# Turning attention probabilities in 32x32 squares on VectorE and through DRAM, and multiplying them with v two subtiles at a time

## What is computed

```python
h = rms_norm(x, ln_g); proj = h @ w_in
# 8 query heads of 64, 2 key/value heads, blocks of 128 tokens, window of 128 keys
scores = einsum('bnqkgd,bnskd->bnkgqs', q * 64**-0.5, keys_of_this_and_previous_block)
scores = where(valid, scores - slope_h * distance, -1e30)
p = softmax(concat([scores, sink_h]))[..., :-1]          # each row sees exactly 128 keys
y_attn = einsum('bnkgqs,bnskd->bnqkgd', p, v) * silu(g_attn)
x = x + concat([y_pool, y_conv, y_attn]) @ w_out
out = rms_norm(x, final_g)
```

## Time and profile before

| | before |
|---|---|
| runs, us | 1399.31, 1399.58, 1400.87 |
| median | 1399.58 |
| the profiled execution's span | 1398.6 (the page gives no other time for it; 1.0 below the median) |
| busy: PE, DVE, ACT, POOL | 1376.3, 1189.1, 553.6, 389.1 us |
| attention stage | 0 to 617 us, eight blocks; blocks 1 to 5 take 73.3 us each |
| memory traffic | 114.27 MB read, 81.79 MB written |

### The profile page before, as it was taken

How to read it: one execution, slowest core, us unless ns; L and a number is a source line. 1 busy time by engine, 2 the same in 40 slices (tenths; PEclk the granted TensorE clock), 3 DMA queues, 4 the chain that set the end, 5 groups by cost and what they waited for, 6 DMA issues and landing times.

```text
span 1398.6 us, 21036 instructions
## 1 busy us (share of the span) xinstructions
PE 1376.3 (98%) x7326; PEld 1131.5 (81%) x7326; DVE 1189.1 (85%) x2480; ACT 553.6 (40%) x1435; POOL 389.1 (28%) x592
## 2 busy tenths in 40 slices
PE   6999999999999999999999999999999999999997
PEld 4888888888888888878888888888888888888886
DVE  5887878796978786769899998988999998898886
ACT  5756565655565654512212122111231333333332
POOL 5133324233242423120101101010010455445551
PEclk9999999999999999999999999999999999999999
DMA  9716070616252426363303213032326484555431
GB/s 216 206 45 257 19 273 19 235 75 207 95 199 103 151 106 210 123 118 153 136 16 136 101 66 135 15 135 101 125 113 260 201 264 161 177 180 171 159 108 74
DMA packets 89385, 197.23 MB, mean 141 GB/s; under 512 B 13904, under 2 KB 55248, under 8 KB 81616
## 3 DMA queue, kind: packets, MB, share of 16 engines
q1 hardware_dynamic: 65152, 172.28, 34.9%
q10 hardware_dynamic: 24144, 23.80, 6.5%
HBM read 114.27 MB, written 81.79 MB: 140 GB/s over the span
## 4 chain that ended last, share of the span: by engine, by line
PE 90%; DVE 7%; DMA 1%; ACT 1%; issue 1%; POOL 0%; SPq 0%; POOLq 0%; DVEq 0%; ACTq 0%
PE wide L346 13%; PE wide L347 13%; PE wide L348 13%; PE pair L1186 6%; PE pair L1187 6%; PE pair L1192 6%; PE wide L1186 4%; PE wide L1187 4%; PE wide L1192 4%; DVE m_tail L1967 3%; PE wide L1224 2%; PE pair L1157 2%; PE turn L1144 2%; PE turn L346 2%; PE pair L346 2%; PE pair L348 2%
## 5 line engine op out<-in xcount | busy, mean ns | idle before, releaser
L1967 DVE SCALAR_TENSOR_TENSOR m_tail<-m_tail,m_taps 128x512 f32<-128x512 f32 x480 | 338.4, 750 | 4.6
L108 POOL TENSOR_TENSOR pool_carrier<-pool_carrier 128x1 f32<-128x1 f32 x77 | 29.5, 383 | 692.0 <-DVE m_meanvar L1976 398.4
L1186 PE MATMUL pair<-xT,w_hi 128*128 128x512 f32 x384 | 154.0, 401 | 4.8 <-DVE w_lo L410 4.6
L1187 PE MATMUL pair<-xT,w_lo 128*128 128x512 f32 x384 | 150.6, 392 | 0.0
L1710 POOL TENSOR_TENSOR operand_sums<-m_y 128x512 f32<-128x512 f32 x75 | 102.0, 1360 | 167.8 <-PE wide L348 116.7
L1192 PE MATMUL pair<-xT,w_hi 128*128 128x512 f32 x384 | 147.1, 392 | 0.0
L787 POOL TENSOR_SCALAR a_rows<-a_rows,a_inv 128x128 f32<-128x128 f32 x256 | 111.4, 453 | 75.3 <-DVE a_inv L993 75.3
L346 PE MATMUL wide<-x_first,w_hi 128*128 128x512 f32 x320 | 125.5, 392 | 0.0
L346 PE MATMUL wide<-xT,w_hi 128*128 128x512 f32 x320 | 125.2, 391 | 0.0
L348 PE MATMUL wide<-x_first,w_hi 128*128 128x512 f32 x320 | 124.6, 389 | 0.0
L347 PE MATMUL wide<-x_first,w_lo 128*128 128x512 f32 x320 | 124.6, 389 | 0.0
(11 more groups left out here) (264 smaller groups left out, 3220.0 us busy)
## 6 DMA issues: line engine op xcount, KB each, us to landing
xT_scratch<-xT SPq DMA_DIRECT2D x16, 2048.0 KB, 8.2
x_first<-xT_scratch SPq DMA_DIRECT2D x16, 1024.0 KB, 7.6
xT<-xT_scratch SPq DMA_DIRECT2D x16, 1024.0 KB, 9.0
combo_scratch<-stage SPq DMA_DIRECT2D x28, 512.0 KB, 4.4
m_y<-y_scratch ACTq DMA_DIRECT2D x14, 1024.0 KB, 6.7
xs<-in_x_dram SPq DMA_DIRECT2D x20, 512.0 KB, 8.1
y_scratch<-y_out SPq DMA_DIRECT2D x8, 1024.0 KB, 4.2
y_scratch<-y_out SPq DMA_DIRECT2D x16, 512.0 KB, 2.9
```

The lines of the kernel that those rows point to most:

```text
L1186: nc.tensor.matmul(out, w.hi(c)[:, kk, cols], st.hi[:, kk, :], start=(kk == 0), stop=False)
L1187: nc.tensor.matmul(out, w.lo(c)[:, kk, cols], st.hi[:, kk, :], start=False, stop=False)
L1967: nc.vector.scalar_tensor_tensor(out=conv[:, i, :], in0=h[:, i, j:j + TB], scalar=taps[:, i, j:j + 1], in1=conv[:, i, :], op0=ALU.mult, op ...
```

## The change

The probabilities of a subtile are no longer turned on PE. Their tile is laid out as four runs of 32 keys, each with all heads. DVE transposes it in place in 32x32 squares (one instruction over 128x1024); SP stores the tile in DRAM (512 KB) and loads it back in four pieces of 32 partitions (128 KB each, runs of 1 KB), which puts the squares in their places. Where a key's row and a query lie in different halves of 64, the row belongs to one of the two key tiles alone and needs no mask. Where they lie in the same half, two instructions a subtile on POOL (rows 0 to 63, `mask_early`) and two on DVE (rows 64 to 127, `mask_late`) multiply with masks, over 512 elements a row each. `attend` takes two subtiles at once (32 matmuls) and writes the two banks `turn`; the products of a block's subtiles 0 and 1 come behind the next block's q0, those of 2 and 3 behind its v. `output` multiplies with the gate while copying, so `gate_output` on POOL and an ACT copy go. The slots o0 to o3 of the pair banks go. v is turned in the scores of subtile 1 instead of 0. SP's queue gets the stores and loads, and two of its other stores swap places. POOL's loop over the blocks is written out. In the last block the products of subtiles 0 and 1 come behind g3, and those of 2 and 3 behind ca0; DVE begins the mixer stage with their output.

```diff
@@ -576,7 +576,7 @@
     rows = sb("rows", [P, 4, D])
     k_hi = sb("k_hi", [P, KV, P + TB], F32R)
     k_lo = sb("k_lo", [P, KV, P + TB], F32R)
-    pT = sb("pT", [P, 2, KV, GROUP * P])
+    pT = sb("pT", [P, 2 * D])
     v = sb("v", [P, 1 + SUB, P])
     q_at = region.at
     q = sb("q", [P, HEADS, TB], F32R)
...
-           tanh.rearrange("p a b -> p (a b)"), pT[:, 0].rearrange("p b c -> p (b c)"), ident, ident_ready, first_rows)
...
+           tanh.rearrange("p a b -> p (a b)"), pT[:, D + D // 2:], ident, ident_ready, first_rows)
+    SQ = 32
+    RUNS = P // SQ
+    probs = [rows[:, b].rearrange("p (s h c) -> p h s c", s=RUNS, h=HEADS) for b in range(2)]
...
+    upper = rows[:, 2:4].rearrange("p a b -> p (a b)")
+    whole = [pT[:, 0:D], upper[:, 0:D]]
+    rest = [pT[:, D:D + D // 2], upper[:, D:D + D // 2]]
+    masks = upper[:, D + D // 2:]
+    earlier_tile, absent = masks[:, 0:P], masks[:, P:2 * P]
+    rest_mask, whole_mask = masks[:, 2 * P:2 * P + HD], masks[:, 2 * P + HD:3 * P]
...
-        use = PAIRED.index(p)
-        return len(PAIRED) // 2 * n + use // 2 - use % 2
+        return len(PAIRED) // 2 * n + PAIRED.index(p) // 2
+    def batches_before(n, batch):
+        return 2 * n + batch
...
+    def store_probs(sp, n, j):
+        m, b = SUB * n + j, j % 2
+        sp.wait_ge(squares_turned, m + 1)
+        need(sp, p_loaded[b], 16 * RUNS * (m // 2))
+        sp.dma_start(p_scratch[b], rows[:, b]).then_inc(p_stored[b], 16)
+    def load_probs(sp, n, j):
+        m, b = SUB * n + j, j % 2
+        sp.wait_ge(p_stored[b], 16 * (m // 2) + 16)
+        need(sp, pv_full, batches_before(n, j // 2))
+        squares = p_scratch[b].rearrange("(a r) (s e) -> s r a e", r=SQ, s=RUNS)
+        for s in range(RUNS):
+            sp.dma_start(whole[b][s * SQ:(s + 1) * SQ].rearrange("r (a e) -> r a e", a=RUNS), squares[s]
+                         ).then_inc(p_loaded[b], 16)
...
+                store_probs(sp, n - 1, 3)
                 st.load(sp, n + 1, (0, 1))
+                for j in (2, 3):
+                    load_probs(sp, n - 1, j)
             st.wait_loaded(sp, n + 1)
             if n == 0:
                 combos.load_raw(sp, 0, [(0, 1), (1, 1), (0, 0), (1, 0)])
             store_xT(n, 0)
             for s in combos.of_block(n, (0, 1)):
                 combos.store(sp, s)
+            store_xT(n, 1)
+            for s in combos.of_block(n, (2, 3, 4)):
+                combos.store(sp, s)
             if n > 0:
                 store(n - 1)
-            for s in combos.of_block(n, (2, 3, 4)):
-                combos.store(sp, s)
-            store_xT(n, 1)
+            for j in (0, 1):
+                store_probs(sp, n, j)
+                load_probs(sp, n, j)
+            store_probs(sp, n, 2)
...
+        for j in (2, 3):
+            load_probs(sp, NB - 2, j)
...
-            m, b = 4 * n + j, j % 2
+            m, b = SUB * n + j, j % 2
             for kv in range(KV):
-                carrier.pool_wait(pool, den_step, 4 * m + 2 * kv + 2)
+                pool.wait_ge(den_step, 4 * m + 2 * kv + 2)
                 for t in range(GROUP):
                     h = kv * GROUP + t
-                    last = nc.gpsimd.tensor_scalar(probs[:, b, h, :], probs[:, b, h, :], inv[:, b, h:h + 1], 0.5,
+                    last = nc.gpsimd.tensor_scalar(probs[b][:, h], probs[b][:, h], inv[:, b, h:h + 1], 0.5,
                                                    ALU.mult, ALU.mult)
                 last.then_inc(probs_ready, 1)
-        def gate_output(n, at):
-            pool.wait_ge(free(at[1]), earlier(*at) + 1)
-            pool.wait_ge(free(slot("o2")), earlier(n, slot("o2")) + 1)
-            for t in range(GROUP):
-                last = nc.gpsimd.tensor_tensor(y[:, t, :], y[:, t, :], gate[:, t, :], ALU.mult)
-            last.then_inc(gated, 1)
+        def mask_early(n, j):
+            m, b = SUB * n + j, j % 2
+            pool.wait_ge(p_loaded[b], 16 * RUNS * (m // 2 + 1))
+            part = runs(whole[b][:, 0:D // 2], halves[0])
+            nc.gpsimd.tensor_tensor(runs(rest[b], halves[0]), part, over_heads(rest_mask, halves[0]), ALU.mult)
+            nc.gpsimd.tensor_tensor(part, part, over_heads(whole_mask, halves[0]), ALU.mult).then_inc(masked, 1)
         def body(n):
-            if isinstance(n, int) and n == 0:
+            if n == 0:
                 make_seen()
-            if not isinstance(n, int) or n < NB - 1:
+            else:
+                mask_early(n - 1, 1)
+            if n < NB - 1:
                 st.root(pool, n + 1, carrier)
-            if not isinstance(n, int) or n > 0:
-                gate_output(n - 1, (n, slot("o3")))
+            if n > 0:
+                for j in (2, 3):
+                    mask_early(n - 1, j)
             for j in range(SUB):
                 normalise(n, j)
-        body(0)
-        with pool.Fori(1, NB - 1) as n:
+                if j == 2:
+                    mask_early(n, 0)
+                    if n == NB - 1:
+                        mask_early(n, 1)
+        for n in range(NB):
             body(n)
-        body(NB - 1)
+        for j in (2, 3):
+            mask_early(NB - 1, j)
...
-        def pT_copy(m, kv):
-            dve.wait_ge(p_turned, 2 * m + kv + 1)
-            if isinstance(m, int) and m == 0:
-                dve.wait_ge(seen_ready, 3)
-            for tile in range(2):
-                last = nc.vector.tensor_tensor(pT[:, tile, kv, :], turn[kv][:], seen[:, tile], ALU.mult)
-            last.then_inc(pT_done, 1)
+        def turn_squares_of_probs(m):
+            dve.wait_ge(probs_ready, 2 * m + 2)
+            nc.vector.transpose(rows[:, m % 2], rows[:, m % 2]).then_inc(squares_turned, 1)
...
-                pT_copy(4 * n - 1, 0)
-                pT_copy(4 * n - 1, 1)
+                turn_squares_of_probs(SUB * n - 1)
+                mask_late(dve, n - 1, 1)
...
+                output(dve, n - 1, 0)
...
                 make_combos(n, (t,) if t < 3 else (3, 4))
+                if t > 1 and not first:
+                    mask_late(dve, n - 1, t)
...
+            if not first:
+                output(dve, n - 1, 1)
             for j in range(SUB):
-                for kv in range(KV):
-                    take_scores(n, j, kv)
-                    if kv == 0 and j:
-                        pT_copy(4 * n + j - 1, 0)
-                        pT_copy(4 * n + j - 1, 1)
+                take_scores(n, j, 0)
+                if j in (1, 2):
+                    turn_squares_of_probs(SUB * n + j - 1)
+                elif j == 3:
+                    mask_late(dve, n, 0)
+                    if final:
+                        mask_late(dve, n, 1)
+                take_scores(n, j, 1)
                 invert(4 * n + j, j % 2, 0)
+                if j == 3:
+                    turn_squares_of_probs(SUB * n + 2)
...
+        turn_squares_of_probs(SUB * NB - 1)
+        output(dve, NB - 1, 0)
+        for j in (2, 3):
+            mask_late(dve, NB - 1, j)
+    def mask_late(dve, n, j):
+        m, b = SUB * n + j, j % 2
+        dve.wait_ge(p_loaded[b], 16 * RUNS * (m // 2 + 1))
+        part = runs(whole[b][:, D // 2:], halves[1])
+        nc.vector.tensor_tensor(runs(rest[b], halves[1]), part, over_heads(rest_mask, halves[1]), ALU.mult)
+        nc.vector.tensor_tensor(part, part, over_heads(whole_mask, halves[1]), ALU.mult).then_inc(masked, 1)
+    def output(dve, n, batch):
+        dve.wait_ge(pv_full, batches_before(n, batch) + 1)
+        if batch == 0:
+            need(dve, y_stored, 16 * n)
+        tokens = lambda a, late: a.rearrange("p g (j l c) -> p l j g c", l=2, c=HD)[:, late, 2 * batch:2 * batch + 2]
+        for late in range(2):
+            last = nc.vector.tensor_tensor(tokens(y, late), turn[late].rearrange("p (s g c) -> p s g c", s=2, g=GROUP),
+                                           tokens(gate, late), ALU.mult)
+        last.then_inc(gated, 1)
...
+    def attend(pe, n, batch):
+        need(pe, gated, batches_before(n, batch))
+        if batch == 0:
+            pe.wait_ge(v_ready, n + 1)
+        subtiles = SUB * n + 2 * batch + 2
+        pe.wait_ge(masked, 2 * subtiles)
+        def product(s, late, kv, odd, tile, keys, start, stop):
+            out = turn[late][halves[odd], (KV * s + kv) * P:(KV * s + kv + 1) * P]
+            turned, first = (rest[s], 0) if keys is halves[late] else (whole[s], 2 * late)
+            weights = turned[keys].rearrange("p (a k t o c) -> p k o t a c", k=KV, t=2, o=2, c=SQ)[:, kv, odd, :, first:first + 2]
+            return nc.tensor.matmul(out, v[keys, 2 * batch + s + tile, halves[kv]], weights, start=start, stop=stop)
+        for s in range(2):
+            for kv in range(KV):
+                for late in range(2):
+                    for odd in range(2):
+                        product(s, late, kv, odd, late, slice(0, P), s == 0 and kv == 0, False)
+        for s in range(2):
+            for kv in range(KV):
+                for late in range(2):
```

(25 more changed lines are left out.)

254 lines of the change are left out of this document (97 added, 157 removed).

## The result

The changed kernel takes 1484.1 us (median of four runs, 1480.9 to 1485.8) against 1400.2 us (1399.3 to 1400.9) beside it on the same chip: 1.059 times as long, 95% interval 1.058 to 1.061. The forecast was slower, 1419 us; the time lies 65 us above it and 46 above the range.

The account below looks back on a forecast made before the run. PE was taken as the bound, DVE a second one with slack of a few tenths at k. 34.8 us removed against 54.5 us of waits gave a span of 1418.3, about 1419 us with 1.0 to the median; range 1389 to 1438.

Parts of the forecast that it names:

- What PE loses: Attention stage: turns gone 28.2 us, last turn's wait 1.0, changes of shape paid once a pair 5.6; 34.8 us removed.
- Wait (a): PE ahead of scores of subtile 3, until DVE has taken subtile 2's: 0.8 us a block, eight blocks, 6 us.
- Wait (b): PE at its last matmul of k, for DVE's last low split: 3.0 us, seven blocks, 21 us.
- Wait (c): Products behind v, for `mask_late` behind the last combination: 4.4 us, blocks 1 to 5, 22 us; block 6 some 1.5.
- Rival 3: Masks run at 1.40 us throughout, waits sum to 76 us: 1441 us; chance 0.06.
- Wait (d): Load of x issued behind the store of subtile 3's tile: 0 to 1.3 us, taken 0.3, six blocks, 2 us.
- Wait (e): End of attention, last products wait for subtile 3's store, load and masks: 2 us, bounds 0 and 5.
- rival 4: Waits of 4.4 us in five blocks could drop PE's clock to 1.2 GHz: 12 us more, 1431 us; chance 0.07.
- The frame: Attention stage goes at the sum of PE's starts, PE busy in 98%; waits are added to that.
- Rival 1: DVE keeps up, turns are simply gone, only the wait at k stays: 1386 us; chance 0.20.
- rival 5: Gains and waits cancel: 1399 us; chance 0.07.
- rival 2: Transfers late, a four-piece load over 7 us delays k; at 10 us some 24 us more, 1443 us; chance 0.06.

## Why the prediction failed

**What PE loses (34.8 us)** stands. No run measures it alone, but PE's busy time rose by 0.7 with 24 us of half clock and, by the estimate above, some 10 of uncounted waiting in it, so some 33 were taken away.

**Wait (a), scores of subtile 3:** 3.8 us for 6 forecast. Right.

**Wait (b), k:** 23.9 us (17.4 + 6.5) for 21. The size was right, the owner only in part: the forecast followed DVE's low splits, and PE waited first for ACT's high ones, behind exponentials behind DVE's scores. Taking 4.9 us a block from DVE did not shorten it. The step priced DVE's work by its instructions and had no term for the 2.0 us a block by which two of them grew beside GpSimd's early masks; that the size came out is partly luck.

**Wait (c), late masks:** 25.9 us for 23.5, but only 19.4 of it at the places that were priced; 6.5 stand ahead of block 7's first products, which had no term. That the sums are so near is luck. The mechanism, masks behind the last combination, is shown by the run that moved them. The masks themselves were priced at 0.75 us and took 0.89 in the mean (57.1 us for 64): 0.69 alone, 1.75 beside GpSimd, as here:
```profile
349.40 1.75 DVE L1188 TENSOR_TENSOR a_rows<-a_rows 64x512 f32<-64x512 f32 x1
351.07 0.68 DVE L1189 TENSOR_TENSOR a_rows<-a_rows 64x512 f32<-64x512 f32 x1
```
```profile
348.06 1.29 POOL L854 TENSOR_TENSOR a_rows<-a_rows 64x512 f32<-64x512 f32 x1
349.31 1.29 POOL L855 TENSOR_TENSOR a_rows<-a_rows 64x512 f32<-64x512 f32 x1
```
Rival 3's price thus holds, and is exceeded, beside GpSimd, but most masks ran alone: 51 of 64 took 0.7 us or less.

**Wait (d), the fold: the first step that failed.** 2 us forecast, 15.0 measured. The step counted the later issue, "0 to 1.3 us", and took 0.3. In block 4 x was issued 1.9 us behind the last split (before 0.03) and landed 15.6 us behind it, before 10.8:
```profile
363.48 0.42 ACT L239 ACTIVATE a_tanh<-xs 128x256 f32<-128x256 f32 x1 [6.18 <-DMA xs<-in_x_dram]
```
That is 4.8 us against 1.3 us of slack: 1.9 by the later issue, which the step saw, and 2.9 by a longer way to landing, which it put at nothing. SP's two loads took 11.5 us in the median where it was 8.1; the step named the half megabyte ahead of them and priced only its issue.

**Wait (e), the end: the second.** 2 us forecast with bounds of 0 and 5, 16.7 measured. The round trip was priced from one 4.4 us transfer; the nine small loads and the weight load ahead of it in SP's queue (670.1 to 681.1 us) were not counted at all, though the weight load's place is in the diff and the small ones stand above it in the kernel. Its masks also run on both engines at once, six of eight at 1.70 to 1.76 us. Moving the two loads ahead gave 8.2 us.

**The half clock: the third, and the largest in the account.** It was rival 4, with 0.07, as if it excluded the forecast; yet the forecast's own waits are what brings it. It belonged into the sum. 24 us were lost for 12 priced, and not only behind the waits of 4 us that rival 4 named. Filling the waits in the changed kernel shows the account's limit: it gives back 7.

**The frame** was the fourth. The forecast added waits to a PE that sets the pace. Ahead of k it no longer does: 19 us of added work there cost 19.2 before and nothing after. The 10 us that the view of waits does not count had no term.

Errors in us of the terms: (a) -2, (b) +3, (c) -4, block 7's first products +6, (d) +13, (e) +15, half clock +24, uncounted waiting +10, together 65 for the 64 by which the span was missed. Rival 1 (DVE keeps up) and rival 5 are refuted; rival 2 was half right: transfers were late, but x's and not the probabilities', whose pieces landed in 4.5 and 3.2 us in the median, though in 6.2 and 6.8 in block 4. How much each term would be worth with all the others mended was not measured for each.

## What to carry to other kernels

When the bound engine has no waits, look at what each of its instructions covers before taking it away: here 2.6 us of turns and products between g3 and k hid the others' chain, and were worth nothing once gone. Price a transfer by what stands ahead of it on its queue, in issues and in bytes, and move the one with the least slack first: putting one x load ahead of one store gave 15.8 us. Once a forecast has waits of 2 to 4 us on TensorE, 1.4 to 3.2 us lost to the half clock behind some of them belong in the sum; but fill them with work only if TensorE is still what the block waits for. When work goes to GpSimd, look at which of VectorE's instructions will stand beside it, small ones on the way to the next stage above all.
